# Recurrence of a hybrid encoder step: score products in a round's last phases, sample states in quarters, filler products in the inverse

## What is computed

```python
def step(S, inp):                         # S: (value, key) state of a head
    r_t, w_t, k_t, v_t, a_t, b_t = inp
    sa = einsum('bhij,bhj->bhi', S, a_t)
    S = S * w_t[:, :, None, :] + sa[..., None] * b_t[:, :, None, :] + v_t[..., None] * k_t[:, :, None, :]
    y = einsum('bhij,bhj->bhi', S, r_t)
    return S, y
```

## Time and profile before

| | us |
|---|---|
| median of 3 runs | 2278.2 (2270.9 to 2286.1) |
| profiled execution | 2273.1 |
| its span, first to last instruction | 2271.3 |
| TensorE, VectorE, ScalarE, GpSimd busy | 2063, 1334, 746, 198 |
| mean granted TensorE clock | 0.926 |

### The profile page before, as it was taken

One profiled execution on the slowest core, in us unless ns is written; L12 is line 12 of the kernel. 1 busy time (PEld: TensorE's weight loads), 2 busy tenths in 40 slices (PEclk: granted clock), 3 DMA queues, 4 the chain that ended last, 5 costly groups with the idle time before them and its releaser, 6 DMA issues.

```text
span 2271.3 us, 37176 instructions
## 1 busy us (share of the span) xinstructions
PE 2063.1 (91%) x15388; PEld 1915.9 (84%) x15388; DVE 1333.9 (59%) x2123; ACT 746.4 (33%) x1290; POOL 198.4 (9%) x199
## 2 busy tenths in 40 slices
PE   2989988888888978989999998999899989999996
PEld 2988876766667758989999998999568989999996
DVE  7675566567666534787436644425574787526754
ACT  3443443233333321422212213322683522112222
POOL 3000223211322100000000000000330000000000
PEclk9999978778788868999999999999999999999998
DMA  2211000000000022122222222241652122222221
GB/s 106 91 58 61 11 1 13 12 3 13 13 11 3 12 75 98 56 75 70 70 86 73 68 70 86 75 158 41 240 182 94 56 75 70 70 84 75 68 70 58
DMA packets 30325, 150.69 MB, mean 66 GB/s; under 512 B 4784, under 2 KB 7600, under 8 KB 17872
## 3 DMA queue, kind: packets, MB, share of 16 engines
q1 hardware_dynamic: 30160, 148.32, 18.9%
HBM read 137.84 MB, written 10.47 MB: 65 GB/s over the span
## 4 chain that ended last, share of the span: by engine, by line
PE 60%; DVE 6%; ACT 2%; issue 1%; DMA 0%; DVEq 0%; POOL 0%; ACTq 0%; SPq 0%; POOLq 0%
PE ps L600 16%; PE ps L602 16%; PE ps L601 16%; PE ps L1925 1%; PE ps L666 1%; PE ps L664 1%; PE ps L665 1%; PE ps L1945 1%; PE ps L1914 1%; PE ps L1324 1%; DVE w_lo L595 1%; DVE split_f L811 1%; DVE gate_e L931 1%; PE ps L1939 1%; PE ps L1909 1%
## 5 line engine op out<-in xcount | busy, mean ns | idle before, releaser
L600 PE MATMUL ps<-x_hi,w_hi 128*128 128x320 f32 x2208 | 694.0, 314 | 67.3 <-DVE x_lo L718 41.3
L601 PE MATMUL ps<-x_lo,w_hi 128*128 128x320 f32 x2208 | 690.5, 313 | 0.0
L602 PE MATMUL ps<-x_hi,w_lo 128*128 128x320 f32 x2208 | 690.0, 313 | 0.0
L600 PEld LDWEIGHTS ps<-x_hi,w_hi 128*128 128x128 f32 x2208 | 422.2, 191 | 72.3 <-issue 46.9
L595 DVE TENSOR_TENSOR w_lo<-raw,w_hi 128x2048 fp32r<-128x2048 f32 (+2 forms) x110 | 229.7, 2089 | 412.7 <-ACT w_hi L589 412.7
L601 PEld LDWEIGHTS ps<-x_lo,w_hi 128*128 128x128 f32 x2208 | 422.4, 191 | 0.2
L602 PEld LDWEIGHTS ps<-x_hi,w_lo 128*128 128x128 f32 x2208 | 421.9, 191 | 0.0
L589 ACT ACTIVATE w_hi<-raw 128x2048 fp32r<-128x2048 f32 (+2 forms) x110 | 192.0, 1745 | 420.9 <-PE ps L602 420.9
L602 PE MATMUL ps<-hid_hi,w_lo 128*128 128x320 f32 x704 | 217.5, 309 | 0.0
L600 PE MATMUL ps<-hid_hi,w_hi 128*128 128x320 f32 x704 | 217.5, 309 | 0.0
L601 PE MATMUL ps<-hid_lo,w_hi 128*128 128x320 f32 x704 | 217.5, 309 | 0.0
(11 more groups left out here) (263 smaller groups left out, 3116.1 us busy)
## 6 DMA issues: line engine op xcount, KB each, us to landing
raw<-in_w_gate SPq DMA_DIRECT2D x22, 1024.0 KB, 4.8
raw<-in_w_up SPq DMA_DIRECT2D x22, 1024.0 KB, 4.9
raw<-in_w_down SPq DMA_DIRECT2D x16, 768.0 KB, 4.2
raw<-in_w_down SPq DMA_DIRECT2D x16, 640.0 KB, 3.9
raw<-in_w_kv SPq DMA_DIRECT2D x8, 1024.0 KB, 4.8
past_k<-in_past_k SPq DMA_DIRECT2D x8, 1024.0 KB, 7.1
past_v<-in_past_v SPq DMA_DIRECT2D x8, 1024.0 KB, 4.9
raw<-in_w_r SPq DMA_DIRECT2D x4, 1024.0 KB, 7.2
```

The lines of the kernel that those rows point to most:

```text
L600: pe.matmul(out, w, x, start=start, stop=False)
L601: pe.matmul(out, w, xl, start=False, stop=False)
L602: return pe.matmul(out, wl, x, start=False, stop=stop)
```

## The change

- Scores. `pe_grams` and `dve_grams` of tile i+1 run in slots 15 to 19 of round i, a block a slot, in banks 4 and 5. Tile 0's run ahead of the rounds. The r factor is made in two pieces.
- The rest of what stood ahead of slot 0 moves into slots: logits, sigmoids, keys and centring to slot 0; one-plus and the first transposes to slot 1; norms, variance, the bonus products and the last transposes to slot 2; the roots to slot 3; norming to slot 4. `act_seeds` moves to slot 19 of the round before. The output of tile i-2 moves to slots 15, 17 and 18.
- Preparation. The reciprocals of `gate_a` come first (slots 2 to 5), those of `sig_w` in 6 to 9, the scan in 10 and 11, all four exponentials in slot 12, the factors in 13 and 14.
- Sample states. `s_ar` is gone: `s_from` takes the two heads as separate 64-row products. `s_state` runs once, in slot 14, as 64x64 quarters of 256 columns in two banks. `s_pre` and `s_out` use one product against the identity instead of two.
- Fillers. `pe_filler` writes a 128x256 product of the identity and a table to a bank that the next products overwrite. It is called for part 0 of each "inv" and each "add" of levels 1 to 6, twelve a tile.
- SyncE starts the load of `low_g2` behind the state transfers instead of ahead of them.

```diff
@@ -418,31 +418,23 @@
     for n in range(NPT):
         for j, step in enumerate(("pre", "u", "out")):
             STEPS[3 * (n + 1) + j].append((step, n))
-    for k, step, hh in ((4, "s_from", 0), (6, "s_pre", 0), (7, "s_u", 0), (9, "s_out", 0),
-                        (10, "s_state", 0), (13, "s_state", 1)):
+    for k, step, hh in ((4, "s_from", 0), (6, "s_pre", 0), (7, "s_u", 0), (9, "s_out", 0), (14, "s_state", 0)):
         STEPS[k].append((step, hh))
 
     def tile_of(f):
         return 0 <= f < NF
 
-    for i in ROUNDS:
-        if i == NF + 1:
-
-            for q in range(4):
-                take(("lin", C_O, q), q)
-        if tile_of(i + 1):
-            take(("zw", i + 1), 4, 2)
-            take(("za", i + 1), 6, 2)
-        if tile_of(i):
-            for u in range(NT):
-                for hh in range(2):
-                    take(("gram", i, hh, u), (2 * u + hh) % 4)
-        if tile_of(i + 1):
-            take(("ss", i + 1), 6, 2)
-        if tile_of(i):
-            take(("bonus", i), 4)
-            for j in range(3):
-                take(("bk_tok", i, j), 4 + (j + 1) % 2)
+    FIRST_GRAM = SLOTS - NT
+    OUTPUT_AT = {15: "y_t", 17: "sv_t", 18: "zg"}
+
+    def gram_plan(f, u):
+
+        for hh in range(2):
+            take(("gram", f, hh, u), 4 + hh)
+
+    for u in range(NT):
+        gram_plan(0, u)
+    for i in ROUNDS[:-1]:
...
@@ -452,11 +444,17 @@
                             take(("add", i, part, hh, n), 2 * part + hh)
                     else:
                         take((phase, i, part, n), 2 * part + (phase == "off"))
-            if tile_of(i - 2) and k == 0:
-                take(("y_t", i - 2), 4, 2)
-                take(("sv_t", i - 2), 6, 2)
-            if tile_of(i - 2) and k == 1:
-                take(("zg", i - 2), 4, 2)
+            if tile_of(i + 1) and k == 0:
+                take(("zw", i + 1), 4, 2)
+                take(("za", i + 1), 6, 2)
+            if tile_of(i) and k == 1:
+                take(("bk_tok", i, 0), 4)
+                take(("bk_tok", i, 1), 5)
+            if tile_of(i) and k == 2:
+                take(("bk_tok", i, 2), 4)
+                take(("bonus", i), 5)
+            if tile_of(i + 1) and k == 2:
+                take(("ss", i + 1), 6, 2)
...
                     elif step in ("pre", "u"):
                         take((step, i - 1, n), 4)
-                    elif n == 0:
+                    elif step == "s_state":
+                        for g, bank in enumerate((4, 7)):
+                            take(("s_state", i - 1, g), bank)
+                    else:
                         take((step, i - 1), 5 if step == "s_out" else 7)
+            if tile_of(i + 1) and k >= FIRST_GRAM:
+                gram_plan(i + 1, k - FIRST_GRAM)
+            if tile_of(i - 2) and k in OUTPUT_AT:
+                take((OUTPUT_AT[k], i - 2), 6, 2)
...
@@ -1196,22 +1205,25 @@
         return v_tok[:, n, f * P + hh * HD:f * P + (hh + 1) * HD]
 
     def pe_rec(pe, i):
-        if tile_of(i + 1):
-            pe_logits(pe, i + 1)
-        if tile_of(i):
-            pe_grams(pe, i, 0, 3)
-        if tile_of(i + 1):
-            pe_norms(pe, i + 1)
-        if tile_of(i):
-            pe_grams(pe, i, 3, NT)
-            pe_by_token(pe, i)
         for k in range(SLOTS):
             if tile_of(i):
                 pe_merge(pe, i, k)
-            if tile_of(i - 2) and k < 2:
-                pe_output(pe, i - 2, k)
+            if tile_of(i + 1) and k == 0:
+                pe_logits(pe, i + 1)
+            if tile_of(i) and k in (1, 2):
+                pe_by_token(pe, i, k)
+            if tile_of(i + 1) and k == 2:
+                pe_norms(pe, i + 1)
             if tile_of(i - 1):
                 pe_states(pe, i - 1, k)
+            if tile_of(i + 1) and k >= FIRST_GRAM:
+                pe_grams(pe, i + 1, k - FIRST_GRAM)
+            if tile_of(i - 2) and k in OUTPUT_AT:
+                pe_output(pe, i - 2, OUTPUT_AT[k])
+
+    def pe_filler(pe, bank, n=2 * P):
+
+        pe.matmul(ps[:, bank, 0:n], ident, table[:, 0:n], start=True, stop=True)
...
+        pe.wait_ge(S("r_made"), 2 * f + (1 if u < NPT - 1 else 2))
+        at = slice(u * P, (u + 1) * P)
+        banks = [claim(pe, ("gram", f, hh, u)) for hh in range(2)]
...
-                pe.wait_ge(S("inv_packed"), 2 * ((len(LEVELS) - 1) * f + n - 1) + part + 1)
                 key = ("inv", f, part, n)
                 bank = claim(pe, key)
+                if part == 0:
+                    pe_filler(pe, bank)
+                pe.wait_ge(S("inv_packed"), 2 * ((len(LEVELS) - 1) * f + n - 1) + part + 1)
...
+                banks = [claim(pe, ("add", f, part, hh, n)) for hh in range(2)]
+                if part == 0 and n:
+                    pe_filler(pe, banks[0])
                 emptied(pe, ("off", f, part, n))
-                banks = [claim(pe, ("add", f, part, hh, n)) for hh in range(2)]
...
@@ -1370,20 +1386,20 @@
                 fill(mm, ("y", f, n))
             elif step == "s_from":
 
-                pe.wait_ge(S("s_ar_made"), f + 1)
                 bank = claim(pe, ("s_from", f))
                 for s in range(NS):
-                    mm = pe.matmul(ps[0:HD, bank, s * 4 * TS:(s + 1) * 4 * TS].rearrange("p (c t) -> p c t", c=4), state_s[:, s, :],
-                                   s_ar[:, :, :, s * TS:(s + 1) * TS].rearrange("p h q t -> p (h q) t"), start=True, stop=True)
+                    for hh in range(2):
+                        rows = slice(hh * HD, (hh + 1) * HD)
+                        mm = pe.matmul(ps[rows, bank, s * 2 * TS:(s + 1) * 2 * TS].rearrange("p (q t) -> p q t", q=2), state_s[rows, s, :],
+                                       ra[rows, b, :, TP + s * TS:TP + (s + 1) * TS], start=True, stop=True)
                 fill(mm, ("s_from", f))
             elif step == "s_pre":
 
                 emptied(pe, ("s_from", f))
                 bank = claim(pe, ("s_pre", f))
+                pe.matmul(ps[:, bank, 0:P], s_from[:, A_OF, :], ident, start=True, stop=False)
                 for hh in range(2):
-                    out = ps[:, bank, hh * HD:(hh + 1) * HD]
-                    pe.matmul(out, s_from[:, hh, A_OF, :], ident[0:HD, 0:HD], start=True, stop=False)
-                    mm = pe.matmul(out, score(f, hh, SAMPLE, "ka"), v_of(f, SAMPLE, hh), start=False, stop=True)
+                    mm = pe.matmul(ps[:, bank, hh * HD:(hh + 1) * HD], score(f, hh, SAMPLE, "ka"), v_of(f, SAMPLE, hh), start=False, stop=hh == 1)
                 fill(mm, ("s_pre", f))
...
+                banks = [claim(pe, ("s_state", f, g)) for g in range(2)]
+                pe.wait_ge(S("spread_made"), f + 1)
+                pe.wait_ge(S("v_spread_made"), f + 1)
+                for q in range(2):
+                    for g, bank in enumerate(banks):
+                        rows = slice(g * HD, (g + 1) * HD)
+                        for hh in range(2):
+                            out = ps[hh * HD:(hh + 1) * HD, bank, 0:HALF_STATES].rearrange("p (s i) -> p s i", s=NS // 2)
+                            mm = pe.matmul(out, bk_tok[rows, b, SAMPLE, q, hh * HD:(hh + 1) * HD], spread[rows, q, hh, :, :],
+                                           start=q == 0, stop=q == 1)
+                        if q:
+                            fill(mm, ("s_state", f, g))
...
     def act_rec(act, i, chain):
-        if tile_of(i + 1):
-            act_sigmoids(act, i + 1)
-        f = i - 2
-        if tile_of(f):
-            act.wait_ge(S("y_centred"), f + 1)
-            act.activation(r_t[:, f, :], k_t[:, f, :], ACT.Square).then_inc(S("y_squared"), 1)
-        if tile_of(i):
-            act_seeds(act, i)
-        act_roots(act, i + 1, i - 2, chain)
-        f = i
-        if tile_of(f):
-            bank = filled(act, ("bonus", f))
-            if f >= 2:
-                act.wait_ge(S("sv_made"), f - 1)
-            read(act.activation(bonus[:, f % 3, :, :], ps[:, bank, 0:2 * NT].rearrange("p (t h) -> p t h", h=2), ACT.Copy), ("bonus", f))
-            for j in range(3):
-                bank = filled(act, ("bk_tok", f, j))
-                nt = min(2, NT - 2 * j)
-                read(act.activation(bk_tok[:, f % 2, 2 * j:2 * j + nt, :, :],
-                                    ps[:, bank, 0:2 * nt * P].rearrange("p (t q n) -> p t q n", t=nt, q=2), ACT.Copy), ("bk_tok", f, j))
         for k in range(SLOTS):
             if tile_of(i):
                 act_blocks(act, i, k)
+            if tile_of(i + 1) and k == 0:
+                act_sigmoids(act, i + 1)
+            if tile_of(i - 2) and k == 1:
+                act.wait_ge(S("y_centred"), i - 1)
+                act.activation(r_t[:, i - 2, :], k_t[:, i - 2, :], ACT.Square).then_inc(S("y_squared"), 1)
+            if tile_of(i) and k in (2, 3):
+                act_by_token(act, i, k)
+            if k == 3:
+                act_roots(act, i + 1, i - 2, chain)
             if tile_of(i - 1):
```

(58 more changed lines are left out.)

260 lines of the change are left out of this document (137 added, 123 removed).

## The result

| | before | after |
|---|---|---|
| median of 20 runs each, side by side, us | 2278.2 | 2263.5 |
| ratio after to before, 95% interval | | 0.9943 (0.9918 to 0.9967) |
| span of the profiled execution, us | 2271.3 | 2259.0 |
| granted clock, mean over the span | 0.926 | 0.943 |

Faster by 0.6%, 14.7 us; forecast was 58. The direction was right, the size four times too large.

A forecast was written before the change was run, and what follows sets the result against it. It took the rounds for a relay between engines with no engine full and a low granted clock. Round 0 +11, 1 -12, 2 to 6 -45, 7 -8, 8 -4 sum to -58: 2273.1 to 2215, median 2220 us, range 2175 to 2288.

The forecast's parts named there:

- The sum at full clock: A full round wholly at 2.4 GHz goes from 64 to 62.3 us, so only -2.
- The clock in rounds 2 to 6: Main gain: granted clock 0.93 instead of 0.80, 9 us at 1.2 GHz costing 3 us; a round becomes 65, -9.
- Why the clock falls: Merge slots: long TensorE waits precede the falls, such as 2.0 us in slot 8 behind two exponentials.
- The fillers: Twelve a round: six inverse fillers lie in waits and cost 0; six add fillers cost 0.45 each, +2.7.
- Rival (b): Slower: at half clock inverse fillers outgrow their waits too, 10.6 a round instead of 2.3; 2315 us; chance 0.12.
- The sample states: Slots 5 to 14: state products in quarters take 1.0 us, -2.7, of which +1.0 returns in slot 14.
- The start: Round 0 pays for tile 0's and tile 1's scores, +11; round 1 has no centring yet, -12.
- The last rounds: Round 7 -8; round 8 -4, with tile 6's output behind the states at +5.
- Rival (a): Clock stays at 0.80 since VectorE relays still leave TensorE idle: 2260 us; chance 0.17.
- Rival (c): VectorE's idle time in the slots swallows most of the moved 14.3 us, another 8 to 9 a round: 2160; chance 0.13.
- (d): In slot 15 TensorE waits for the A and R factors, 3 us longer than walked: 2244 us; chance 0.08.
- the prediction's rule: VectorE instructions with two SBUF inputs and GpSimd ones reading SBUF exclude each other: centring's subtraction took 2.12 us against 0.83.

The follow-up runs named there:

- a_bonus_only: Changed kernel with only the five bonus products of a tile moved from slot 2 to slot 19: 2236.1 us, 0.9816 of the kernel before.
- a_tile0: Changed kernel with only tile 0's ten scores put on all eight banks in turn, in place of two: 2247.0 us, 0.9837 of the kernel before.
- a_end: Changed kernel with only its last round put in another order: 2256.4 us, 0.9893 of the kernel before.
- a_no_fillers: Changed kernel without any of its filler products: 2342.4 us, 1.0245 of the kernel before.
- b_fillers: Kernel before with only the twelve fillers a tile added: 2289.4 us, 1.0045 of the kernel before.
- a_all: Changed kernel with slot 2 reordered, bonus in slot 19, last round reordered and tile 0's scores on eight banks: 2183.6 us.
- a_slot2: Changed kernel with slot 2 reordered (norms first, third transposes on bank 5) and bonus products in slot 11: 2232.7 us, 0.9774.
- a_again: The changed kernel itself, unaltered, measured once more with a second profile: 2263.1 us, 0.9945 of the kernel before.

## Why the prediction was wrong, step by step

The forecast missed by 45.7 us between the profiled executions: 23.6 in rounds 7 and 8, 20.7 in rounds 2 to 6, 8.0 up to tile 2, less the 6.7 that the rest gave. Two steps failed. In rounds 2 to 6 it is the account of the clock: how much of a round stands at 1.2 GHz, what its falls stand behind, and what raises it. At the tail it is the walk through the last round.

**The sum at full clock: near, 1 us low.** 62.3 us a round were forecast. The changed kernel has no full round wholly at full clock, but a_bonus_only has one of 61.9 at 1.00 (slots 0 to 4, 5 to 14 and 15 to 19: 17.6, 28.0 and 16.4, where 19.0, 28 and 15.4 were forecast). It has no bonus products in slot 2; there they cost 1.5 us at full clock (slot 2 of round 1, all at 1.00: 4.8 us in a_tile0 and a_end, 3.3 in a_bonus_only). With them the changed kernel's order comes to 63.4, an estimate from these rows. That VectorE and TensorE alternate on banks 4 and 5, and that next round's off 0 waits for the last mask (1.49), came as said.

**The clock in rounds 2 to 6: the amount was mis-sized.** The forecast was 0.93, 9 us of a round at 1.2 GHz, at 0.3 lost for each: 3 us. Measured: 0.90, that is 20% of 68.25 us or 13.7 us at 1.2 GHz, and they cost 68.25 - 63.4 = 4.9, 0.35 each. So the price of one was about right, and by luck: the working had 0.53 from the earlier trace rows and then took 0.3 without a row for it. What was wrong is how much stands at the low clock. The 13.7 us lie in slots 2 to 5, where the forecast placed bonus and norm products "where it has no wait to fill" and priced them at the earlier trace rows's full clock; that the change adds 1.06 and 1.26 us of waiting for bank 4 beside them (ScalarE reads the bank behind its inv_n) was not seen. The five rounds came to 343.2 us in place of 325: 5.5 of the 18 from the full-clock sum, 9 from the clock, the rest from round 2 (70.1) and from rounding 65.3 to 65.

**Why the clock falls: read from the wrong wait.** The prediction named, as the longest of three waits that explain the fall in the kernel before, the 2.0 us ahead of slot 8 behind two exponentials, and took it for one "in front of the falls". The windows of the same stretch have the clock down before that wait began:

```profile
407.00:407.60 0.60, 0.60 (x12) 0.60 (x14) 0.60 (x5) 0.00 (x0) 0.00 (x0) 1.00 0.00 0
407.60:410.60 3.00, 3.00 (x20) 2.70 (x18) 2.97 (x9) 0.28 (x1) 0.00 (x0) 0.51 0.00 0
410.60:412.63 2.03, 0.01 (x1) 0.00 (x0) 0.02 (x1) 1.99 (x5) 0.00 (x0) 0.50 0.00 0
```

It fell at 407.6, in the first products of slot 7; the wait began at 410.6. And the cure, taking the exponentials out of slot 7, does not hold the clock by itself: a_no_fillers has it and stays at 0.50 through slots 5 to 14 in four of the five full rounds.

**The fillers: costed as work, not for what they do.** They stood at 0 for six and 2.7 for the other six. The prediction named them beside the long waits that go as a reason for the higher clock, and gave them no term of their own: without fillers the same order of work ends at 2342, 79 us later. The price of the add fillers was right per piece (0.43 to 0.50 against 0.45) and too high in sum (1.6 against 2.7). Rival (b) did not come about in the changed kernel, where the clock rose. Its cost is real where the clock stays low: in rounds 4 to 6 of b_fillers.

**The sample states: the row was read for its duration only.** -1.7 a round was forecast from the earlier trace rows. The new products are as short as estimated, 1.09 us for all in slot 14. But the profile of before held, in the same rows, that the first pair runs at half clock and the second at full, and the clock comes back between them: the change took away what stood at that rise. Alone that cost 0.3%.

**The start: +8, nearly all of it in round 1.** Tile 0's scores and round 0 were put at +11 and are +12.1 (10.97 and 47.5 before, 14.4 and 56.2 after). Round 1 was put at -12, from 71.2, and is 66.1 at 0.87. In a_tile0 and a_end it is 59.4 at 1.00: the forecast's number, reached when the clock holds.

**The last rounds: +24, the largest part.** Tile 6's output behind the states was put at +5 and is 11.7 with the wait for x_lo; ScalarE's roots and weight splitting ahead of u (4.05) were not walked through; and the stretch ran at 0.52 where it was 0.68. The step that failed took the gain of 11.0 us at the head of round 8 as if nothing more than these 5 came back at another place in the same chain. With both put in order (a_all) the stretch is 13.4 us shorter at nearly the same clock.

**The untouched rest: -6.7.** The forecast had 0. It goes with 17 us less at half clock there, whose reason stays open.

Rival (a) named a time close to the result, 2260, but not for its reason: the clock did rise, to 0.90. Rival (c) did not show: the walk through slots 0 to 4, 19.0, is what they take at full clock (17.6 and the bonus products' 1.5). Nor did (d): TensorE's wait for VectorE's A factor in slot 15 is 1.0, not 3. Of the signs that the prediction set, round 0 near 57 (56.2) and slots 15 to 19 came as said, rounds of 62 to 67 and slots 0 to 4 near 19 did not (68.3 and 23.0), and neither did its signs of being wrong, rounds above 71 or slots 15 to 19 above 20. It had set none for the tail, where the largest part was missed.

## What to carry to other kernels

In a chain of small products, first find from narrow windows when the granted clock rose and when it fell, and what TensorE did before that; a wait that stands after the fall is not its cause. A change that removes what stood at the rises can cost more than its own time says. Work moved out of a visible stall must be checked for the bank that it takes over and for who reads that bank last: here moving five products of two columns gave 27 us of 2263, and changing the bank and the order beside them as well gave 53. And walk the last round by itself: what leaves its head comes back at its tail unless it has idle time to go to.

## What the runs showed of the hardware

- TensorE busy by the profile and clock are two things: 5.68 of 5.68 us at 0.50 (kernel before), 40.1 of 42.5 us at 0.50 (a_no_fillers), and 16.76 of 16.76 at 0.59 beside the same instructions in 12.06 at 1.00 (a_slot2, 13.6 us of it at 0.50 without a gap). The Trainium skill ("TensorE: Matmul & The Clock Gate", "What's actually happening") describes the full clock as what activity releases; by the profile's busy time alone that can't be seen here, since a stretch that is all busy stayed at 1.2 GHz until wider products came.
- The bonus products of a_slot2 took the same 1.18 us in slot 11 of rounds 3 and 5, at full clock both times; the clock fell at their end in one (they start at 487.66) and not in the other (616.63). Equal rounds need not get equal clocks.
- Twelve filler calls a tile, which shorten a slot by 0.43 to 0.50 us at full clock when one is left out, kept ten slots at 0.97 that ran at 0.50 without them: 28.8 against 42.5 us. On the kernel before they raised the clock in rounds 0 to 3 and not in rounds 4 to 6.
- The clock's pattern can repeat from round to round and in a second execution (68.25, 68.25, 68.31, 68.24 us; 68.27, 68.27, 68.27, 68.31 in the second profile), and yet another kernel with the same instructions up to the last round had 70.5 to 77, and the ten executions of a_again lie 27 us apart.
- Centring's subtraction took 2.12 us after the change too, with a GpSimd product of 1.54 starting beside it (537.27 and 537.37). The same line took 0.83 in round 7 (741.14), where no GpSimd product ran beside it. This is what the prediction's rule says; no run moved the GpSimd product away.
